# Decode stick-breaking units: the probabilities are turned five pieces behind the scores in place of four, values and outputs one piece later

## The reference, cut to what matters

```python
def sb_attend(q, k, v, q_pos, k_pos):
    z = jnp.einsum("bqhd,bkhd->bhqk", q, k) * (HEAD_DIM ** -0.5)
    mask = k_pos[None, :] < q_pos[:, None]
    log_1m = jnp.where(mask, jax.nn.log_sigmoid(-z), 0.0)
    suffix = lax.cumsum(log_1m, axis=3, reverse=True) - log_1m
    a = jnp.where(mask, jnp.exp(jax.nn.log_sigmoid(z) + suffix), 0.0)
    return jnp.einsum("bhqk,bkhd->bqhd", a, v)
```

## Time and profile before

| | us |
| --- | --- |
| median of 3 runs | 1031.59 (1030.63 to 1035.68) |
| the profiled execution's own time | 1031.72 |
| its span (first to last instruction) | 1030.0 |
| PE busy | 991.3 |
| DVE busy | 661.5 |
| ACT busy | 462.6 |
| POOL busy | 279.6 |
| data moved by the DMA engines | 234.02 MB, 227 GB/s on average |

### The profile page before, as it was taken

The page is one execution under the profiler, slowest core; times in us unless marked ns, Lnnn a source line. Parts: engine busy times, 40 slices in busy tenths (PEclk is TensorE's granted clock), DMA queues, the critical chain, the costliest instruction groups (busy, mean ns, idle before and its releaser), DMA issues.

```text
span 1030.0 us, 27299 instructions
## 1 busy us (share of the span) xinstructions
PE 991.3 (96%) x11204; PEld 856.4 (83%) x11204; DVE 661.5 (64%) x982; ACT 462.6 (45%) x912; POOL 279.6 (27%) x293
## 2 busy tenths in 40 slices
PE   6999999999999999999999998999988999999997
PEld 5998788987779898899888997887777888887785
DVE  5577446555565566566555624777778777887487
ACT  5522311222123232222332224776887778887453
POOL 2200000000000011011210110531376566666497
PEclk9999999999999999999999999999998999999999
DMA  7358797789999798778988768656444242421443
GB/s 289 111 211 283 254 340 284 305 326 349 351 325 355 294 351 341 284 291 307 386 316 299 282 187 279 167 133 165 115 101 103 62 103 71 104 63 50 143 169 139
DMA packets 121473, 234.02 MB, mean 227 GB/s; under 512 B 60552, under 2 KB 91272, under 8 KB 103952
## 3 DMA queue, kind: packets, MB, share of 16 engines
q1 hardware_dynamic: 96016, 209.33, 58.9%
q10 hardware_dynamic: 25344, 23.08, 6.5%
HBM read 204.52 MB, written 27.86 MB: 226 GB/s over the span
## 4 chain that ended last, share of the span: by engine, by line
PE 81%; POOL 6%; DVE 5%; issue 4%; ACT 2%; DMA 1%; DVEq 0%; POOLq 0%; ACTq 0%; SPq 0%
PE bank L899 31%; PE bank L886 9%; PE bank L968 7%; PE bank L1011 6%; PE bank L1755 6%; PE bank L1262 5%; PE bank L1238 5%; PE bank L1215 4%; PE bank L996 3%; DVE pr L1499 2%; PE bank L1193 1%; PE bank L1277 1%; POOL o_nat L1930 1%; POOL m_stat L1917 1%; POOL zb L1840 1%
## 5 line engine op out<-in xcount | busy, mean ns | idle before, releaser
L899 PE MATMUL bank<-w_hi,hT_hi 128*128 128x256 f32 (+1 forms) x896 | 259.4, 289 | 1.4 <-DVE hT_lo L625 1.1
L899 PE MATMUL bank<-w_lo,hT_hi 128*128 128x256 f32 (+1 forms) x896 | 253.1, 282 | 0.9 <-issue 0.9
L899 PE MATMUL bank<-w_hi,hT_lo 128*128 128x256 f32 (+1 forms) x896 | 253.0, 282 | 0.0
L899 PEld LDWEIGHTS bank<-w_hi,hT_hi 128*128 128x128 f32 x896 | 170.6, 190 | 5.7 <-issue 3.3
L899 PEld LDWEIGHTS bank<-w_hi,hT_lo 128*128 128x128 f32 x896 | 170.6, 190 | 1.0 <-issue 1.0
L899 PEld LDWEIGHTS bank<-w_lo,hT_hi 128*128 128x128 f32 x896 | 170.9, 191 | 0.1
L536 ACT ACTIVATE u_out<-bank 128x256 f32<-128x256 f32 x112 | 43.0, 384 | 258.3 <-PE bank L899 258.0
L743 DVE STREAM_TRANSPOSE k_buf<-k_buf 128x2048 f32<-128x2048 f32 x64 | 146.2, 2298 | 14.4 <-DMA k_buf<-in_cache_fox_k 7.5
L1620 POOL TENSOR_TENSOR pr<-pr,om 128x1023 f32<-128x1023 f32 (+3 forms) x64 | 93.6, 1468 | 68.0 <-DVE om L1510 49.2
L1238 PE MATMUL bank<-ident,pr 128*128 128x128 f32 x576 | 86.8, 278 | 4.8 <-POOL pr L1620 2.2
L1215 PE MATMUL bank<-k_hl,q_hh 128*128 128x512 f32 x192 | 77.5, 404 | 8.6 <-DVE rowmax L1499 5.3
(11 more groups left out here) (217 smaller groups left out, 1943.9 us busy)
## 6 DMA issues: line engine op xcount, KB each, us to landing
k_buf<-in_cache_fox_k SPq DMA_DIRECT2D x32, 1024.0 KB, 10.2
v_ring<-in_cache_fox_v SPq DMA_DIRECT2D x32, 1024.0 KB, 9.3
k_buf<-in_cache_sb_k SPq DMA_DIRECT2D x32, 1024.0 KB, 10.1
v_ring<-in_cache_sb_v SPq DMA_DIRECT2D x32, 1024.0 KB, 8.9
w_raw<-in_w_in SPq DMA_DIRECT2D x14, 1024.0 KB, 9.3
out<-u_out ACTq DMA_DIRECT2D x72, 128.0 KB, 5.9
q_scratch<-u_out ACTq DMA_DIRECT2D x64, 128.0 KB, 7.2
k_nat<-out SPq DMA_DIRECT2D x32, 256.0 KB, 4.2
```

The costliest lines, as they stand in the source:

```text
L899: mm = pe.matmul(bank[:, U + i % 2, w_cols(c)], a[:, k, hcols(s)], b[c % 2][:, k, w_cols(c)], start=(k == 0 and n == 0), stop=(k == KD - 1 ...
```

## The change

For n >= DB `turn_p` stands five pieces behind the scores in place of four. `VALUES_AT` is made from it (two later), `FRESH_AT` from that, and `TURN_O_AT` from that (two later), so for units 10 to 15 values, fresh and turn_o come one piece later as well; for units 8 and 9 values do, while their fresh and turn_o keep the places set by hand (100 and 102, 103 and 104). Values of unit n now stand at the same i as the scores of unit n + 1, ahead of them. Units 0 to 7 keep all their places. The places of pieces, scores, turn_k, current, of the loads and of the splits don't change. Nothing is added or taken out.

```diff
         SCORES_AT = [29 + 7 * n for n in range(NU_D)]
-        TURN_P_AT = [s + (3 if n < DB else 4) for n, s in enumerate(SCORES_AT)]
+        TURN_P_AT = [s + (3 if n < DB else 5) for n, s in enumerate(SCORES_AT)]
         VALUES_AT = [s + 2 for s in TURN_P_AT]
         EARLY = (0, 1, DB)
         TURN_P_AT[2], VALUES_AT[2] = 46, 49
```

## The result

| | before | after |
| --- | --- | --- |
| median of 6 runs each, us | 1031.25 (1030.30 to 1035.68) | 1040.84 (1039.25 to 1042.10) |
| ratio after / before, 95% interval | | 1.0084, [1.0071, 1.0097] |
| span of the profiled execution | 1030.0 | 1039.0 |
| PE busy | 991.3 | 993.9 |
| last piece ends at | 626.3 | 634.9 |

What follows compares the result with a forecast made beforehand. PE's own work was taken as the bound of the stretch; 1031.7 - 0.7 - 1.2 + 0.4 + 0 = 1030.2 us, own range 1029.0 to 1031.0, wider range 1028.4 to 1033.0.

Steps and rivals of the forecast that it cites:

- What bounds the kernel: From unit 8's scores to the last piece, PE's own work is the bound, busy 252.38 of 254.70 us.
- only 2.3 us of idle time: In that same stretch of PE, no more than 2.3 us could be won by filling idle time.
- a rival as something that might vanish by chance: PE's issue waits, 0.9 us and 1.74 ahead of the first prompt scores, go too: 1027.6 us, chance 0.09.
- Part 1, POOL: Turning a piece later in units 8 to 15 removes PE's 0.7 us wait for POOL in unit 12.
- Part 2, touching: Values of units 8 to 14 run straight into the next scores, saving seven returns to the full array: 1.2 us.
- the bound of 0.36 for a dearer direct step: Fresh straight to scores costs 0.36 us more than the entry it replaces: +1.3, 1032.7 us, chance 0.13.
- the term of -1.2: Between values and the next scores, seven returns to the full array at 0.17 us each go away.
- Part 3, the queues: Later v loads delay k by up to 2.9 us, holding DVE's d_pT copies and PE's values: 0.4 us cost.
- the 0.4 us forecast for unit 11: In unit 11 the d_pT copies end at 489.1, values are due at 488.7, so PE waits 0.4 us.
- Part 4, the end: The last unit's later values delay the first head's query loads, but this is covered: cost 0, at most 1 us.
- The slower one: Late k loads hold turn_k of chunk 2, the d_pT copies and PE's values: 1040 us, chance 0.08.

## Why the prediction was wrong, point by point

- **What bounds the kernel.** That PE's own work is the bound in the stretch was right, but not that only 2.3 us of idle time were left in it: the kernel without v loads needs 250.67 us for it, 4.2 less, since half of each stall stands in rows as busy PE. The step that failed is the sentence on the "issue" waits: 0.9 us "for which the profile shows no releaser". I left them without a cause, gave them to a rival as something that might vanish by chance, and never asked what could make them more. They were the first sign of the mechanism that set the result. The DMA view named the queue that brings the instructions.
- **Part 1, POOL.** Right: the 0.7 us went, and with the slower transpose behind it about 1.1 us in all. The price was read wrongly: "in the seven other units the price and the gain are zero". In unit 8 the transposes covered the wait for w_lo, and their removal cost 1.2 us of wait and 0.3 in the piece behind. A step that is moved was asked what it waits for, but not what it hides.
- **Part 2, touching.** The saved return was there (values to scores without a gap, 0.18 us a unit), and the bound of 0.36 for a dearer direct step held. But the term of -1.2 compared array shapes and not instruction rates, and the supply of instructions stood in the sum at nothing. The piece between values and scores was priced at 0.17 us of overhead; it was also 2.87 us in which PE uses 48 instructions. Without it the scores lost 7.8 us, six times the gain.
- **Part 3, the queues.** The v loads were followed to the k loads and from there to DVE, and DVE did wait longer for k (3.91 us for chunk 2 of unit 11, where it had been 1.02):

```profile
488.76 2.31 DVE L743 STREAM_TRANSPOSE k_buf<-k_buf 128x2048 f32<-128x2048 f32 x1 [3.91 <-DMA k_buf<-in_cache_sb_k]
```

  But this sign came by luck. Chunk 2 is turned 16.2 us behind the end of unit 11's scores (488.76 - 472.54), where it was 16.0 (482.42 - 466.39): k came 0.2 us later there and not 2.9. DVE waits longer because the d_pT copies, which stood ahead of that row, now stand behind it. They end 2.2 us before PE's values are due, and the 0.4 us forecast for unit 11 isn't in the trace. The queue that mattered, the one with the instructions, was not on the list.
- **Part 4, the end.** Right: the first prompt scores start 3.3 us behind the last piece, as before.
- **The rivals.** The slower one gave 1040 us, which is nearly the result, but by k loads and d_pT; its mechanism didn't happen. So neither the sign nor the size was right for a reason that was named.

Shown by runs: the loss is in touching values and scores, it needs the v loads in flight, and the stalls follow the instruction blocks. Only read from traces: the lower clock, and its 1.6 us from one. It doesn't follow every stall: in the one with values alone moved the clock is at 0.50 from 404.3, 472.6, 506.7 and 544.3, behind waits of 0.95, 1.11, 2.61 and 1.55 us, while it stays at 1.00 behind the 0.96 us of unit 9 in the changed kernel and the 1.44 us of unit 9 in the version with one v chunk during values. Open: when a stall brings the clock down, and what holds a small packet back for as long as 1 MB takes.

## What to carry to other kernels

Read an "issue" wait of PE beside the DMA view's instruction packets: if it ends about the same time behind one in every place (here 2.2 to 2.6 us), PE waits for its program. The cost is more than the row says, here about twice. More dense small matmuls in a row, or more data transfers at that moment, made it worse. Keep long matmuls between two bursts of small ones, or move bulk loads out of the time in which the block for the second burst is fetched; here a gate on SP turned the loss of 0.7% of touching values and scores into a gain of 0.2%. And when a step moves, ask which wait it was covering where it stood.

## What the runs showed of the hardware

- PE's instructions come in packets of 16 KB over the same DMA engines as the data. From packet to first use it took 2.2 to 2.6 us in every stall in the scores, and with 1 MB transfers in flight the packet moved 2.0 to 3.1 us later. The time from packet to use isn't contention: in the version with one v chunk during values PE stands still from 402.10 to 403.53 while the DMA engines move nothing (0 GB/s).
- PE goes from products of 128 x 32 directly to 32 x 32 without a gap in the chain, and a single full-array matmul between them cost 0.26 us with its changes of shape.
- While PE waits for instructions, matmuls in flight still count as busy: in unit 9 none started for 1.55 us, the row says 0.96, and the unit lost 2.0.
- A stall of 1.28 us at a full load of work was followed by 3.4 us at a granted clock of 0.50, worth 1.6 us. One of 1.44 us in another version was not.
